# Eight-head attention with two branches: two heads and one branch a turn, in row and column halves

## The reference, cut to what matters

```python
kc = compress(k_cmp, pe_k, ck1, ck2)       # 31 compressed keys and values a group
p_c = softmax(q @ kc * scale - slope * dist_c)
o_c = p_c @ vc
o_s = softmax(masked q @ k_sel * scale - slope * dist) @ v_sel    # selected blocks
o_w = softmax(masked q @ k_win * scale - slope * dist) @ v_win    # window of 512
o = g0 * o_c + g1 * o_s + g2 * o_w         # gates g = sigmoid(...), one a token, head, branch
y_conv = silu(layer_norm(conv31(a * sigmoid(gate)))) @ w_conv_br
x = x + (g_a * (o @ w_attn_br) + g_b * y_conv) @ w_out
```

## Time and profile before

| | |
|---|---|
| median of 3 runs | 2105.08 us |
| profiled execution | 2104.95 us |
| its span, first to last instruction | 2102.9 us |
| PE busy | 2012.3 us (96%) |
| DVE, ACT, POOL busy | 971.3, 741.5, 736.2 us |
| mean granted PE clock | 0.976 of full speed |

### The profile page before, as it was taken

How to read it: one execution, slowest core, us unless ns; L and a number is a source line. 1 busy time by engine, 2 the same in 40 slices (tenths; PEclk the granted TensorE clock), 3 DMA queues, 4 the chain that set the end, 5 groups by cost and what they waited for, 6 DMA issues and landing times.

```text
span 2102.9 us, 22710 instructions
## 1 busy us (share of the span) xinstructions
PE 2012.3 (96%) x9072; PEld 1594.9 (76%) x9072; DVE 971.3 (46%) x1638; ACT 741.5 (35%) x1195; POOL 736.2 (35%) x311
## 2 busy tenths in 40 slices
PE   6888999999999998999999998998998999999998
PEld 4656888888886776888888887876555788888887
DVE  5654454442036544454442027955443665555301
ACT  4444432222245443432222233234454344333222
POOL 2321434444441232434444442422000344444442
PEclk9999999999999999999999999987999999999999
DMA  3410322232231221322232232211000222223322
GB/s 138 146 55 31 110 71 92 98 100 92 99 110 61 91 81 62 109 70 92 99 100 92 99 110 88 93 60 51 20 21 20 71 100 90 101 91 100 100 90 90
DMA packets 51816, 178.60 MB, mean 85 GB/s; under 512 B 5472, under 2 KB 5488, under 8 KB 51456
## 3 DMA queue, kind: packets, MB, share of 16 engines
q1 hardware_dynamic: 45264, 163.07, 23.3%
q10 hardware_dynamic: 6448, 14.09, 1.9%
HBM read 175.00 MB, written 6.33 MB: 86 GB/s over the span
## 4 chain that ended last, share of the span: by engine, by line
PE 84%; DVE 9%; ACT 4%; issue 1%; DMA 1%; POOL 1%; DVEq 0%; ACTq 0%; SPq 0%
PE bank L381 23%; PE bank L383 22%; PE bank L382 22%; PE bank L404 2%; PE bank L469 2%; PE bank L455 1%; DMA raw<-stream 1%; PE bank L1010 1%; DVE tmp L1852 1%; PE bank L1004 1%; PE bank L1005 1%; PE bank L1241 1%; PE bank L1255 1%; PE bank L804 1%; ACT whi L365 1%
## 5 line engine op out<-in xcount | busy, mean ns | idle before, releaser
L370 POOL TENSOR_TENSOR wlo<-raw,whi 128x1024 fp32r<-128x1024 f32 x287 | 688.5, 2399 | 1323.6 <-ACT whi L365 1323.6
L365 ACT ACTIVATE whi<-raw 128x1024 fp32r<-128x1024 f32 x287 | 304.3, 1060 | 921.0 <-PE bank L383 894.7
L381 PE MATMUL bank<-hh,whi 128*128 128x512 f32 x1392 | 555.1, 399 | 32.8 <-DVE hl L512 16.9
L382 PE MATMUL bank<-hl,whi 128*128 128x512 f32 x1392 | 547.1, 393 | 0.0
L383 PE MATMUL bank<-hh,wlo 128*128 128x512 f32 x1392 | 547.0, 393 | 0.0
L381 PEld LDWEIGHTS bank<-hh,whi 128*128 128x128 f32 x1392 | 264.8, 190 | 102.5 <-issue 25.2
L382 PEld LDWEIGHTS bank<-hl,whi 128*128 128x128 f32 x1392 | 264.7, 190 | 56.2 <-issue 2.2
L383 PEld LDWEIGHTS bank<-hh,wlo 128*128 128x128 f32 x1392 | 264.4, 190 | 56.2
L489 DVE TENSOR_TENSOR tmp<-bank,rs 128x512 f32<-128x512 f32 x159 | 108.6, 689 | 242.0 <-PE bank L383 227.7
L381 PE MATMUL bank<-fh,whi 128*128 128x512 f32 x496 | 192.9, 389 | 0.0
L382 PE MATMUL bank<-fl,whi 128*128 128x512 f32 x496 | 192.9, 389 | 0.0
(11 more groups left out here) (263 smaller groups left out, 2551.6 us busy)
## 6 DMA issues: line engine op xcount, KB each, us to landing
raw<-stream SPq DMA_DIRECT2D x307, 512.0 KB, 3.4
bias_scratch<-rel_scratch ACTq DMA_DIRECT2D x1, 4096.0 KB, 17.7
biasB<-bias_scratch ACTq DMA_DIRECT2D x16, 256.0 KB, 2.8
x<-x_in SPq DMA_DIRECT2D x2, 1024.0 KB, 10.1
w<-w_in ACTq DMA_DIRECT2D x2, 1024.0 KB, 5.9
out<-y ACTq DMA_DIRECT2D x8, 256.0 KB, 2.1
cst<-consts_in ACTq DMA_DIRECT2D x1, 577.5 KB, 7.7
gn<-gains_in ACTq DMA_DIRECT2D x1, 318.5 KB, 4.9
```

What stands on the lines that cost most here:

```text
L365: e.activation(slot[u][0][:, :], raw[u % 2][:, :], ACT.Copy).then_inc(*w_hi.done(u))
L370: e.tensor_tensor(slot[u][1][:, :], raw[u % 2][:, :], slot[u][0][:, :].bitcast(F32), ALU.subtract)\
L381: e.matmul(o, wh, h, start=first, stop=False)
L382: e.matmul(o, wh, l, start=False, stop=False)
```

## The change

The attention of the last block takes two heads and one branch a turn: 8 turns i = 2p + br. It uses the pair helpers of the layer before, now with banks and tile order as arguments. Each turn of PE is: scores, the product with V of the turn before (`c_product_pe`, with the compressed product where that turn closed a pair), one whole unit of projection from `C_UNITS` into bank 5, the transposes, and the compressed branch's scores (even turns) or transposes (odd turns). DVE's turn is minima, normalisation, the unit's eviction, and the compressed branch; ACT's turn is exponents, copies, the compressed part, one rounding. The four last gates' Sigmoids come after all turns. The compressed scores take both heads in one matmul, with keys in two halves filled up with zeros (`kcz`). The output's high part moves from ACT to DVE (`c_out_dve`).

In front, the first branch's keys and values and the first queries are projected between the layer norm's sums and the compressions, and the second branch's values move into the first turn. ACT's and DVE's orders follow, with the second Gelu behind the scaling. The merge starts with the convolution branches of its first two tiles.

```diff
                 yield tile_at("w_in", c0 + 2 * CONV_C + (3 * c + j) * P)
-        for s in range(6):
+        for s in range(4):
             yield tile_at("w_in", 512 + s * P)
         yield tile_at("w_in", 0)
+        for s in range(4, 6):
+            yield tile_at("w_in", 512 + s * P)
         for p in range(PAIRS_C):
             if p + 1 < PAIRS_C:
                 yield tile_at("w_in", (p + 1) * P)
...
-    biasC = sb("biasC", [P, T], Y + 10 * KB)
-    probsC = [sb("probsC0", [P, 1280], C + 4 * KB), sb("probsC1", [P, 1280], C + 14 * KB), sb("probsC2", [P, 1280], R4)]
+    biasC = [sb(f"biasC{h}", [P, T], C + 2 * KB * h) for h in range(2)]
+    probsC = [sb("probsC0", [P, 1280], C + 4 * KB), sb("probsC1", [P, 1280], R4)]
...
             for i, (at, w) in enumerate(((0, 512), (512, 512), (1024, 256))):
-
-    def pair_times_v_pe(e, n, vf, PTs, first=True, last=True):
-        e.wait_ge(*spread.at((n, 1, 2)))
-        for k in range(QT):
+                e.activation(PTs[h][:, at:at + w], bank[banks[h][i]][:, 0:w], ACT.Copy).then_inc(*spread.done((n, h, i)))
+
+    def pair_times_v_pe(e, n, vf, PTs, banks=TURNED_IN, first=True, last=True):
+
...
+        project(e, 4, hh, hl, ("kd", 0))
         e.wait_ge(*formed.at(("conv", 3)))
         for c in range(4):
             pe_sum(e, 7, zc[:, c, :], c == 0, c == 3, ("zc", c))
+        e.wait_ge(*made.at("gtok"))
+        project(e, 5, hh, hl, ("vC", 0))
         compress_pe(e, 0)
+        e.wait_ge(*evicted.at(("gate", 10)))
+        project(e, 3, hh, hl, ("qC", 0))
         for c in range(4):
             e.wait_ge(*squared.at(("zc", c)))
             pe_sum(e, 7, tmp[c % 2][:, :], c == 0, c == 3, ("zc2", c))
         compress_pe(e, 1)
-        for br in range(2):
-            e.wait_ge(*evicted.at(("kd", 0, 1) if br else ("cmp", 0)))
-            project(e, 0, hh, hl, ("kd", br))
-            e.wait_ge(*evicted.at(("vC", 0) if br else ("cmp", 1)))
-            project(e, 1, hh, hl, ("vC", br))
-            pe_token_major(e, ("vC", br), tmp[6])
-        project(e, 3, hh, hl, ("qC", 0))
+        e.wait_ge(*evicted.at(("cmp", 0)))
+        project(e, 0, hh, hl, ("kd", 1))
+        e.wait_ge(*evicted.at(("vC", 0)))
+        c_values_pe(e, 0, 1)
         e.wait_ge(*made.at(("hid", 1)))
         e.matmul(bank[2][:, 0:2 * N_CMP], gg("w2k", 0, P), hid[0][:, 0:2 * N_CMP], start=True, stop=True)\
             .then_inc(*mixed.done("kc"))
-        e.wait_ge(*evicted.at("kc"))
+        e.wait_ge(*evicted.at(("kc", 1)))
...
-        compress_act(e, 0)
         for c in range(4):
             e.wait_ge(*formed.at(("centred", c)))
             if c >= 2:
                 e.wait_ge(*summed.at(("zc2", c - 2)))
             act_square(e, tmp[c % 2], zc[:, c, :], ("zc", c))
+            if c == 1:
+                round_unit(e)
+                branch_act(e, 0)
+                compress_act(e, 0)
+        round_unit(e)
+        act_root(e, rs[2], ("zc2", 3))
+        round_unit(e)
         compress_act(e, 1)
-        branch_act(e, 0)
-        act_root(e, rs[2], ("zc2", 3))
-        branch_act(e, 1)
...
+        branch_act(e, 1)
+        c_values_act(e, 0, 1)
         round_unit(e)
...
+        branch_dve(e, 0, 4)
...
+        e.wait_ge(*proj.at(("vC", 0)))
+        e.wait_ge(*made.at(("kp", 1, 3)))
+        dve_scale(e, 5, rs[0], tmp[6][:, :], ("vC", 0))
         compress_dve(e, 0)
-        compress_dve(e, 1)
-        branch_dve(e, 0)
+        e.wait_ge(*proj.at(("qC", 0)))
+        dve_scale(e, 3, rs[0], qC[0][:, :], ("qC", 0))
...
-        branch_dve(e, 1)
+        compress_dve(e, 1)
...
-        e.wait_ge(*proj.at(("qC", 0)))
-        dve_scale(e, 3, rs[0], qC[0][:, :], ("qC", 0))
+        branch_dve(e, 1, 0)
...
+        e.memset(kcz[:, :, :, :], 0.0).then_inc(*formed.done("zero_k"))
         e.wait_ge(*mixed.at("kc"))
-        e.tensor_copy(kcd[:, :, 0:N_CMP], bank[2][:, 0:2 * N_CMP].rearrange("p (g n) -> p g n", g=2))\
-            .then_inc(*evicted.done("kc"))
+        e.wait_ge(*formed.at("zero_k"))
+        for h in range(2):
+            r = slice(64 * h, 64 * h + 64)
+            e.tensor_copy(kcz[r, h, :, 0:N_CMP], bank[2][r, 0:2 * N_CMP].rearrange("p (g n) -> p g n", g=2))\
+                .then_inc(*evicted.done(("kc", h)))
...
 
 
-    NC_ = 4 * PAIRS_C
+
+
...
+        for t in C_ORDER:
+            if i:
+                e.wait_ge(*spread.at((("C", i - 1), 1, {0: 0, 2: 0, 3: 1, 1: 2}[t])))
+            for h in range(2):
+                bk, c = PAIR_SPOT[h, t]
+                r = slice(64 * h, 64 * h + 64)
+                e.matmul(bank[bk][:, c:c + W(t)], qC[p % 2][r, t * P:(t + 1) * P], kd[br][p // 2][r, 0:W(t)],
+                         start=True, stop=True).then_inc(*scored.done((("C", i), h, bk)))
...
+    def c_product_pe(e, i):
+        p, br = i // 2, i % 2
+        if br:
+            e.wait_ge(*spread.at(("cmp", p)))
+            e.matmul(bank[7][:, :], vcb[p // 2][:, :], tmp[6][0:64, :], start=False, stop=False, skip_group_check=True)
+        elif p:
+            e.wait_ge(*low.at(("C", p - 1)))
+        else:
+            e.wait_ge(*spread.at(("vC", 1)))
+        pair_times_v_pe(e, ("C", i), lambda k, h: vC[br][:, k, 64 * (p // 2):64 * (p // 2) + 64], PTB, C_TURNED_IN, br == 0, br == 1)
 
     def compressed_front_pe(e, p):
-        if p == 0:
-            e.wait_ge(*evicted.at(("vc", 1, 1)))
-        else:
-            e.wait_ge(*evicted.at(("qC", p)))
...
+        for i in range(NC_):
+            p, br = i // 2, i % 2
+            c_scores_pe(e, i)
+            if i:
+                c_product_pe(e, i - 1)
+            if br:
+                e.wait_ge(*evicted.at(("cmp_scores", p)))
+            elif p:
+                e.wait_ge(*spread.at(("cmp", p - 1)))
+            project(e, 5, hh, hl, C_UNITS[i])
+            pair_transposes_pe(e, ("C", i), probsC, C_TURNED_IN)
+            e.wait_ge(*evicted.at(C_UNITS[i]))
+            if i == 0:
+                c_values_pe(e, 1, 7)
+            if br == 0:
+                compressed_front_pe(e, p)
             else:
-                pe_transposes(e, ("C", n), ORDER, pb)
-            if n < 0:
-                continue
-            if n % 4 == 0:
                 compressed_back_pe(e, p)
-                if p + 1 < PAIRS_C:
-                    u = next_unit(e)
-                    e.wait_ge(*evicted.at(("cmp_scores", p, 1) if p == 0 or p % 2 else ("gate", 11 + p)))
-                    half_unit(e, 3 + (p + 1) % 2, u, 0, None)
-                compressed_product_pe(e, p)
-            elif n % 4 == 1 and p + 1 < PAIRS_C:
-                half_unit(e, 3 + (p + 1) % 2, u, 1, ("qC", p + 1))
-            elif n % 4 == 2:
-                u = next_unit(e)
-                e.wait_ge(*evicted.at(("cmp_scores", p + 1, 1) if p + 1 < PAIRS_C else ("gate", 14)))
-                half_unit(e, 3, u, 0, None)
-            elif n % 4 == 3:
-                half_unit(e, 3, u, 1, ("gate", 12 + p))
-            pe_times_v(e, ("C", n), lambda k: vC[br][:, k, 64 * (p // 2):64 * (p // 2) + 64], 64 * h, 64 * h + 64, False, n % 4 == 3)
+        c_product_pe(e, NC_ - 1)
...
+        for i in range(NC_):
+            p, br = i // 2, i % 2
+            for h in range(2):
+                if i:
+                    e.wait_ge(*stats.at(((("C", i - 1), h), "inv")))
+                act_exp(e, (("C", i), h), probsC[h], 16 * h, C_ORDER)
+            if i:
+                e.wait_ge(*mixed.at(("C", i - 1)))
+            pair_spread_act(e, ("C", i), PTB, C_TURNED_IN)
+            if i == 0:
+                c_values_act(e, 1, 7)
+            if br == 0:
+                compressed_exp_act(e, p)
+            else:
                 compressed_back_act(e, p)
+            round_unit(e)
+        for j in range(12, 16):
+            gate_act(e, j)
...
+        for i in range(NC_):
+            p, br = i // 2, i % 2
+            for h in range(2):
+                if br == 0:
+                    e.wait_ge(*formed.at(("biasC", p, h)))
+                if i:
+                    e.wait_ge(*turned.at((("C", i - 1), h, 2)))
+                pair_mins_dve(e, ("C", i), h, probsC[h], biasC[h], SCALE_B, C_ORDER)
+            if i == 0:
+                e.wait_ge(*made.at("gtok"))
+            for h in range(2):
+                at = 3 * (2 * p + h) + 1 + br
+                dve_normalise(e, (("C", i), h), probsC[h], 16 * h, gtok[:, :, at:at + 1].rearrange("p t a -> p (t a)"), C_ORDER)
+            c_unit_dve(e, C_UNITS[i])
+                    c_out_dve(e, p - 1)
+                compressed_scores_dve(e, p)
+            else:
+                compressed_norm_dve(e, p)
+                if p + 1 < PAIRS_C:
+                    c_bias_dve(e, p + 1)
+        c_out_dve(e, PAIRS_C - 1)
+
+    def c_out_dve(e, p):
+        e.wait_ge(*mixed.at(("C", 2 * p + 1)))
+        e.tensor_scalar(oh[:, p, :], bank[7][:, :], 1.0, None, ALU.mult).then_inc(*formed.done(("C", p, "high")))
+        e.wait_ge(*formed.at(("C", p, "high")))
```

(7 more changed lines are left out.)

231 lines of the change are left out of this document (79 added, 152 removed).

## The result

The changed kernel takes 2028.27 us (four runs, 2026.5 to 2029.41), the one before 2105.1 beside it: ratio 0.9636, interval 0.962 to 0.9653. That is 77 us less; 2030 was forecast. The profiled execution has a span of 2025.5 us at a mean granted clock of 0.987, where it was 2102.9 at 0.976.

A forecast was written before the change was run, and what follows sets the result against it. TensorE (PE) was taken as the bound, 84% of the path that ends last. Front 56.9 plus attention 115.5 gave 172.4 against 247.6 us, 75 less: 2030 us, range 2019 to 2050.

The forecast's parts named there:

- PE's durations: Attention turns: two-head scores 2.36 us, products 2.30, transposes 2.10, compressed scores 0.9; a pair 27.2 where it was 43.4.
- The reason given for the pairing: Attention turns: neighbouring matmuls in different halves of the array run beside each other, and only neighbours do.
- the forecast's 5.0 us a turn: Attention turns: gain from pairing two heads, 2.74 us in scores and 2.30 in products with V.
- pairs don't overlap: Rival, attention turns: paired heads don't run beside each other, 5.04 us x 8 more, 2070 us; chance 0.03.
- The softmax is hidden: Attention turns: softmax takes 9.3 of the 10.3 us before the first transpose, leaving 1 us to spare.
- The rival's mechanism: Softmax shows: PE waits 1.5 us a turn at transposes, perhaps as much again in clock; 2042 to 2056 us; chance 0.11.
- The first rival: Attention turns: the clock falls once a turn, at transposes and compressed scores, losing 1.7 us x 8; 2044 us; chance 0.13.
- the half-clock one: Rival, attention turns: half clock throughout, every turn doubles, 2133 us, slower than before; chance 0.03.
- First and last turn: Attention's ends: first turn 16.1 us with scores at half clock; 4.9 us after the eighth, including a 1.5 us wait.
- The front's chain: Front, from the sums of squares on, paced by DVE and ACT: 22.5 us where it was 23.7, bounds 19 and 27.
- The 7.5 us for the front: Front of the last block's attention: 56.9 us in all, 7.5 less, for one unit fewer.
- 1447 was named as a sign: Start of the attention: first scores near 1447 would show the forecast right.

The follow-up runs named there:

- e1_heads_in_turn: Changed kernel with each turn's scores, and the product with V, issued for all of head 0 and then head 1 instead of alternating; 2044.14 us, ratio 0.9704.
- e6_dose_large: Changed kernel with 18 extra small VectorE multiplications in each turn, between head 0's last exponent and its normalisation; 2066.41 us, ratio 0.9824.
- e7_pool_beside: Changed kernel with one GpSimd weight rounding held back to run beside VectorE's four scalings in the front instead of ahead of them; 2029.6 us, ratio 0.9638.

## Why the prediction was right

- **PE's durations**, taken from the layer before, held to 0.1 us: 2.36 and 2.30 as forecast, transposes 2.18 for 2.10, compressed scores 0.93 for 0.9. The pair is 27.64 us for 27.2. Odd turns took 0.6 us more than forecast, half of it the 0.30 us wait for the compressed probabilities, which the sum left out.
- **The reason given for the pairing was half of it.** `e1_heads_in_turn` gives 2.5 us of an odd turn and 1.7 of an even one to the overlap of neighbours, 17 us in all. The rest of the forecast's 5.0 us a turn is there without it; that it comes from the single block is argued from rows. So the rival "pairs don't overlap" was priced too high: 2070 forecast, 2044 measured. The duration was taken whole from the layer before, so the sum did not need the reason, and came out right in spite of it.
- **The softmax is hidden**, with more to spare than the forecast's 1 us: normalised 8.97 us after the scores start in turn 1 (forecast 9.3), and a dose of 2.4 us cost under 2 us in the whole kernel, since the sum took all transposes to need both heads. The rival's mechanism is real: beyond the cover the wait is paid and, in `e6_dose_large`, a slow stretch behind it. (That rival's upper end, 2056, should be 2054 by its own terms.)
- **The clock** stays at 1.00 from 1451.4 to the end of the last turn, with 20 transposes in each turn. The first rival and the half-clock one did not happen.
- **First and last turn**: the first takes 13.5 us for 16.1. The prediction read from the earlier trace rows that scores do not bring the clock back; here it came back at 1451.3, when PE had issued only two-head scores since 1447.31, and not in the unit. The last product waits 0.68 us for 1.5.
- **The front's chain was the term mis-sized**: 22.5 us forecast, 20.2 measured (1427.15 to 1447.31, inside the bounds of 19 and 27). The old chain of 23.7 us, from which it was taken, holds the scalings at 4.7 us, where POOL held them up; they take 2.50, and with POOL beside them again (`e7_pool_beside`) the chain is 22.3 (1426.87 to 1449.19). A second step got shorter too: from the mean to the reciprocal it is 1.70 us (1427.15 to 1428.85) where it was 3.41 (1430.30 to 1433.71), as a rounding and the copy of `vC` no longer stand ahead of the root on ScalarE. The forecast gives no terms for these steps, so how much of this second one it had in its 22.5 stays open. The work ahead of it was 34.0 us for 34.4. The 7.5 us for the front were 10.3, of which 5.65 is the unit that moved out.

The forecast had the turns 2 us too short, and the ends and the front 6 us too long. These errors partly cancel, and 2 us of spread outside the stage bring 2028 beside 2030. The first scores at 1447.31, where 1447 was named as a sign, are such a coincidence: the front was 2.8 us shorter than forecast and began 3.0 us later.

## What to carry to other kernels

Where two operations use half of the array, put both in one block and alternate them; alternating gave half of the gain here, and by the rows the block the other half. Put a whole unit of independent matmuls between a softmax's scores and its transposes, and count the slack at the last consumer of the chain: when the clock falls behind a wait, PE pays it nearly twice (24 us of waits and 17 of clock in `e6_dose_large`). Before taking over a VectorE duration, look at what GpSimd did beside it. Spread a block of one-column products among wide ones; that hides none of their time, but the clock held.
